# Root mean square of the output heads in a hybrid layer: column sums by matmul with tokens on partitions, instead of sums spread over channels

## The reference

```
y = jnp.concatenate([y_a, y_b, y_c, y_d.astype(x.dtype)], axis=-1).reshape(b, L, N_OUT_HEADS, HEAD_DIM)
y = rms_norm(y, w['out_norm'].reshape(N_OUT_HEADS, HEAD_DIM)).reshape(b, L, D_MIX)
x = x + g2 * (y @ w['w_out'])
```

## Time and profile before

| | |
|---|---|
| median of 3 runs | 2008.23 us (2001.43 to 2008.45) |
| profiled execution, its own time | 2006.56 us |
| span of that execution | 2004.7 us, so 1.9 us lie around it |
| mean granted TensorE clock | 0.915 of full speed |
| the stage of the norm, first layer | about 700 to 764 us |
| the same, second layer | about 1649 to 1709 us |

### The profile page before, as it was taken

One profiled execution on the slowest core, in us unless ns is written; L12 is line 12 of the kernel. 1 busy time (PEld: TensorE's weight loads), 2 busy tenths in 40 slices (PEclk: granted clock), 3 DMA queues, 4 the chain that ended last, 5 costly groups with the idle time before them and its releaser, 6 DMA issues.

```text
span 2004.7 us, 27629 instructions
## 1 busy us (share of the span) xinstructions
PE 1791.1 (89%) x11432; PEld 1520.4 (76%) x11432; DVE 978.6 (49%) x1755; ACT 585.5 (29%) x778; POOL 206.3 (10%) x373
## 2 busy tenths in 40 slices
PE   4888899999886899899997999989988688899998
PEld 2788888666664656799997999956766365589998
DVE  2443342356666673444435544235765756344443
ACT  2432331114221232433324433111423122244331
POOL 3000001520012400000000000062002140000000
PEclk8899999999866899899998999999986778989999
DMA  8545444867101156345442454484410115225442
GB/s 269 170 162 188 167 168 147 265 211 252 46 14 38 39 187 212 105 127 168 149 146 92 142 164 142 140 233 150 133 42 17 34 40 168 84 85 168 129 160 74
DMA packets 206089, 271.99 MB, mean 136 GB/s; under 512 B 11527, under 2 KB 182072, under 8 KB 205964
## 3 DMA queue, kind: packets, MB, share of 16 engines
q1 hardware_dynamic: 191760, 249.48, 37.7%
q0 software_dynamic: 13328, 20.65, 4.1%
q10 hardware_dynamic: 876, 0.09, 0.0%
HBM read 264.68 MB, written 5.50 MB: 135 GB/s over the span
## 4 chain that ended last, share of the span: by engine, by line
PE 77%; DVE 12%; DMA 6%; ACT 2%; issue 1%; ACTq 1%; SPq 1%; DVEq 0%
PE bank L764 14%; PE bank L766 14%; PE bank L765 14%; PE bank L873 10%; DMA sqk<-in_w_ada_dram 5%; PE bank L1262 4%; PE bank L1004 3%; PE bank L698 2%; PE bank L1159 2%; PE bank L997 1%; PE bank L1023 1%; PE bank L1171 1%; DVE big L2140 1%; PE bank L688 1%; DVE sq L2197 1%
## 5 line engine op out<-in xcount | busy, mean ns | idle before, releaser
L766 PE MATMUL bank<-hT_r,ring_r 128*128 128x320 f32 x1408 | 443.1, 315 | 0.0
L766 PEld LDWEIGHTS bank<-hT_r,ring_r 128*128 128x128 f32 x1408 | 269.8, 192 | 0.0
L764 PE MATMUL bank<-hT_r,lat_pages_r 128*128 128x320 f32 x704 | 220.9, 314 | 13.8 <-DVE gates_r L1592 13.6
L1575 DVE TENSOR_TENSOR ring_r<-ring,lat_pages_r 128x2048 fp32r<-128x2048 f32 (+1 forms) x68 | 151.5, 2230 | 149.5 <-ACT lat_pages_r L1288 149.5
L873 PE MATMUL bank<-hT,ring 128*128 128x320 f32 x736 | 214.4, 448 | 10.2 <-DVE hT L1588 10.2
L765 PE MATMUL bank<-gates_r,lat_pages_r 128*128 128x320 f32 x704 | 221.1, 314 | 0.0
L766 PE MATMUL bank<-big_r,ring_r 128*128 128x320 f32 x704 | 218.0, 310 | 0.0
L873 PEld LDWEIGHTS bank<-hT,ring 128*128 128x128 f32 x736 | 142.0, 196 | 73.4 <-issue 21.4
L1288 ACT ACTIVATE lat_pages_r<-ring 128x2048 fp32r<-128x2048 f32 (+1 forms) x68 | 126.5, 1862 | 128.0 <-PE bank L766 64.6
L764 PEld LDWEIGHTS bank<-hT_r,lat_pages_r 128*128 128x128 f32 x704 | 135.3, 192 | 19.6 <-issue 16.7
L765 PEld LDWEIGHTS bank<-gates_r,lat_pages_r 128*128 128x128 f32 x704 | 135.5, 192 | 0.0
(11 more groups left out here) (522 smaller groups left out, 3228.9 us busy)
## 6 DMA issues: line engine op xcount, KB each, us to landing
ring<-in_w_ffn_in_dram SPq DMA_DIRECT2D x88, 1024.0 KB, 5.4
ring<-in_w_ada_dram SPq DMA_DIRECT2D x56, 1024.0 KB, 5.4
ring<-in_w_ffn_out_dram SPq DMA_DIRECT2D x32, 1024.0 KB, 5.2
ring<-in_w_in_dram SPq DMA_DIRECT2D x22, 1024.0 KB, 7.3
sqk<-in_w_ada_dram SPq DMA_DIRECT2D x32, 512.0 KB, 8.5
ring<-in_w_ffn_out_dram SPq DMA_DIRECT2D x16, 768.0 KB, 4.7
lat_pages<-in_cache_mla_latent_dram POOLq DMA_DIRECT2D x128, 64.0 KB, 2.2
ring<-in_w_out_dram SPq DMA_DIRECT2D x8, 1024.0 KB, 8.1
```

The source lines that it names most:

```text
L764: mm(out, w_h, x_h, start=start, stop=False)
L766: return mm(out, w_l, x_h, start=False, stop=stop)
L1575: go(v.tensor_tensor(slot_r(n, nk, 256), slot(n, nk, 256), w_hi_r[g % HI][:, 0:nk].bitcast(F32), ALU.subtract), w_low)
```

## The change

The sums of a head are formed with tokens on partitions, for all chunks at once. `head_sums` makes the squares the stationary operand (128 channels x up to 128 tokens) and the two indicator columns `rows64` (128x2) the moving one, so that one small matmul gives two sums for every token: 22 such matmuls in part 0 and 2 in part 1 (the sample tokens of the last two chunks). The 48 columns of results lie in one bank. ACT takes the root with scale and eps in the same instruction (`head_root`), DVE takes the reciprocal of at most 128x32 values (`head_invert`), and `head_spread` brings the factors back to channels: the stationary operand is one factor column broadcast to 64 columns, the moving one the identity, six matmuls to a chunk. `scale` then reads the factor out of PSUM, chunk by chunk, in the ten parts of `SPREAD`. `BATCH` stays for the squares. The places of the steps in the streams of PE, ACT and DVE move as shown.

```diff
--- before.py
+++ after.py
@@ -94,14 +94,16 @@
 
 BATCH = [(0, 0, T), (2, 0, T), (4, 0, T), (6, 0, TP), (6, TP, T)]
 
+SPREAD = [(k, 0, T) for k in range(6)] + [(6, 0, TP), (7, 0, TP), (6, TP, T), (7, TP, T)]
+
 
 PER = {"states_loaded": 16 * 11, "pages_loaded0": 1024, "pages_loaded1": 1024, "proj_loaded": 16 * 7, "stored": 16 * 16,
        "stored_rows": 16 * 4, "turned": 2, "turned_used": 2, "out_ready": 5, "win_done": 25, "win_act": 10, "win_dve": 15,
        "conv_done": 1, "silu_conv": 1, "ssd_act_in": 3, "ssd_act": 6, "ssd_pe": 7, "ssd_dve": 8, "lru_pe": 2, "lru_act": 3,
        "lru_dve": 2, "hg_e": 8, "hg_bc": 8, "hg_pe": 9, "hg_dve": 7, "mla_pe": 12, "mla_act": 2, "mla_dve": 10,
        "cq_copied": 1, "att_t": 8, "att_tc": 8, "att_k": 32, "att_sq": 32, "att_in": 8, "att_rk": 8, "att_mix": 8,
-       "soft_pe": 12, "soft_dve": 20, "soft_act": 4, "group_used": 4, "on_pe": 5, "on_sq": 5, "on_inv": 5, "on_root": 5,
-       "on_scaled": 5, "wo_done": 8, "wo_used": 8, "mla_act_in": 2, "mla_root": 2, "prob_act": 8, "wkr_ready": 1,
+       "soft_pe": 12, "soft_dve": 20, "soft_act": 4, "group_used": 4, "on_pe": 2, "on_sq": 5, "on_inv": 2, "on_root": 2, "on_spread": 10,
+       "on_scaled": 10, "wo_done": 8, "wo_used": 8, "mla_act_in": 2, "mla_root": 2, "prob_act": 8, "wkr_ready": 1,
        "acol_taken": 1, "mixed": 5}
 
 
@@ -266,6 +268,8 @@
         pend = carve(ext, 1920, 2, NBLK + NB)
         kv_tok = carve(conv, 0, 3, 512)
         hg_s0 = carve(conv, 1536, 2, NB, 64)
+
+        head_inv = carve(ext, 0, KD, 3, 2)
 
         cq = carve(cqkr, 0, 2, T)
         ckv = carve(cqkr, 640, T)
@@ -422,6 +426,7 @@
         on_sq = sem("on_sq")
         on_inv = sem("on_inv")
         on_root = sem("on_root")
+        on_spread = sem("on_spread")
         on_scaled = sem("on_scaled")
         wo_done = sem("wo_done")
         wo_used = sem("wo_used")
@@ -1193,15 +1198,30 @@
                     from_states(1, 0).then_inc(hg_pe, 1)
                     from_states(2, 1).then_inc(hg_pe, 1)
 
-                    def out_norm(n):
-
-                        pe.wait_ge(on_sq, at(on_sq, n + 1))
-                        if n:
-                            pe.wait_ge(on_inv, at(on_inv, n))
-                        k0, c0, c1 = BATCH[n]
-                        for k in range(k0, k0 + 2):
-                            ins = mm(bank[2 + k % 2][:, c0:c1], c("ones64"), sqx[:, k, c0:c1], start=True, stop=True)
+                    def head_sums(part):
+
+                        pe.wait_ge(on_sq, at(on_sq, (4, 5)[part]))
+                        for k in range(0, KD) if part == 0 else (6, 7):
+                            for cc, (t0, L) in enumerate(TC):
+                                if part == (k > 5 and cc == 2):
+                                    ins = mm(bank[2][0:L, 6 * k + 2 * cc:6 * k + 2 * cc + 2], sqx[:, k, t0:t0 + L], c("rows64"),
+                                             start=True, stop=True)
                         ins.then_inc(on_pe, 1)
+
+                    def head_spread(*parts):
+
+                        for i in parts:
+                            k, c0, c1 = SPREAD[i]
+                            pe.wait_ge(on_inv, at(on_inv, 1 + i // 8))
+                            if i >= 2:
+                                pe.wait_ge(on_scaled, at(on_scaled, i - 1))
+                            for cc, (t0, L) in enumerate(TC):
+                                if c0 <= t0 < c1:
+                                    for h in range(2):
+                                        ins = mm(bank[2 + k % 2][64 * h:64 * h + 64, t0:t0 + L],
+                                                 head_inv[0:L, k, cc, h:h + 1].to_broadcast([L, 64]), c("ident", L)[:, 0:L],
+                                                 start=True, stop=True)
+                            ins.then_inc(on_spread, 1)
 
 
                     tail_tiles, tail_steps = iter(TAIL[l]), sorted({step for step, _ in TAIL[l]})
@@ -1216,21 +1236,21 @@
 
                     soft_turn(2)
                     soft_spread(2)
-                    out_norm(0)
+                    head_sums(0)
                     tail(1)
                     value(2)
                     value_taken(2)
                     turn(6)
-                    out_norm(1)
+                    head_spread(0, 1)
                     tail(1)
                     score(6)
                     tail(2)
-                    out_norm(2)
+                    head_spread(2, 3)
                     turn(7)
                     tail_turn(0)
                     tail(1)
                     score(7)
-                    out_norm(3)
+                    head_spread(4, 5)
                     tail(4)
                     soft_turn(3)
                     tail_turn(1)
@@ -1239,18 +1259,19 @@
                     tail(1)
                     value(3)
                     value_taken(3)
+                    head_spread(6, 7)
                     for h in range(4):
                         r = slice(64 * (h % 2), 64 * (h % 2) + 64)
                         ins = mm(bank[7][r, (h // 2) * 64:(h // 2) * 64 + 64], wukv[:, 1, h * 64:(h + 1) * 64],
                                  pn.rearrange("p b (h t) -> p b h t", h=4)[:, :, h], start=True, stop=True)
                     ins.then_inc(mla_pe, 1)
                     tail(3)
-                    out_norm(4)
+                    head_sums(1)
                     tail(2)
                     tail_turn(2)
-
-
-                    pe.wait_ge(on_scaled, at(on_scaled, 5))
+                    head_spread(8, 9)
+
+                    pe.wait_ge(on_scaled, at(on_scaled, 10))
                     for m in range(KD):
                         tile_ready(pe, pos["wout", l, m // 2])
                         w = slot(pos["wout", l, m // 2], 8, 256)
@@ -1517,29 +1538,31 @@
                         ac.wait_ge(mixed, at(mixed, n + 1))
                         o.go(f(batch(sqx, n), batch(hT, n), ACT.Square), on_sq)
 
-                    def on_sqrt(n):
-                        ac.wait_ge(on_inv, at(on_inv, n + 1))
-                        o.go(f(batch(sqx, n), batch(sqx, n), ACT.Sqrt), on_root)
+                    def head_root(part):
+                        ac.wait_ge(on_pe, at(on_pe, part + 1))
+                        sums = bank[2][:, 0:48].rearrange("p (k c h) -> p k c h", k=KD, c=3)
+                        if part == 0:
+                            o.go(f(head_inv[:, :, 0:2], sums[:, :, 0:2], ACT.Sqrt, bias=eps, scale=1.0 / 64))
+                            o.go(f(head_inv[0:64, 0:6, 2], sums[0:64, 0:6, 2], ACT.Sqrt, bias=eps[0:64], scale=1.0 / 64), on_root)
+                        else:
+                            o.go(f(head_inv[0:64, 6:8, 2], sums[0:64, 6:8, 2], ACT.Sqrt, bias=eps[0:64], scale=1.0 / 64), on_root)
 
                     for n in range(4):
                         on_square(n)
                     soft_exp(2)
-                    on_sqrt(0)
+                    head_root(0)
                     att_copy(6)
-                    on_sqrt(1)
                     att_squares(6)
                     att_root(6)
                     tail_copy(0)
                     att_copy(7)
-                    on_sqrt(2)
                     att_squares(7)
                     att_root(7)
                     tail_copy(1)
                     soft_exp(3)
-                    on_sqrt(3)
                     on_square(4)
                     tail_copy(2)
-                    on_sqrt(4)
+                    head_root(1)
                     tail_copy(3)
                     for k in range(KD):
                         square(3 * l + 2, k)
@@ -2188,47 +2211,43 @@
                         o.tell(mixed)
 
 
-                    def invert(n):
-                        k0, c0, c1 = BATCH[n]
-                        ve.wait_ge(on_pe, at(on_pe, n + 1))
-                        for k in range(k0, k0 + 2):
-                            go(v.tensor_scalar(sqx[:, k, c0:c1], bank[2 + k % 2][:, c0:c1], 1.0 / 64, EPS, MUL, ADD))
-                        o.settle()
-                        go(v.reciprocal(sqx[:, k0:k0 + 2, c0:c1], sqx[:, k0:k0 + 2, c0:c1]), on_inv)
-
-                    def scale(n):
-                        k0, c0, c1 = BATCH[n]
-                        ve.wait_ge(on_root, at(on_root, n + 1))
-                        for k in range(k0, k0 + 2):
+                    def head_invert(part):
+                        ve.wait_ge(on_root, at(on_root, part + 1))
+                        if part == 0:
+                            go(v.reciprocal(head_inv[:, :, 0:2], head_inv[:, :, 0:2]))
+                            go(v.reciprocal(head_inv[0:64, 0:6, 2], head_inv[0:64, 0:6, 2]), on_inv)
+                        else:
+                            go(v.reciprocal(head_inv[0:64, 6:8, 2], head_inv[0:64, 6:8, 2]), on_inv)
+
+                    def scale(*parts):
+                        for i in parts:
+                            k, c0, c1 = SPREAD[i]
```

(21 more changed lines are left out.)

## The result

The changed kernel takes 2025.91 us (median of five runs, 2021.08 to 2026.94), the kernel before 2008.23 us beside it (2001.43 to 2009.84). The ratio is 1.009, 95% interval 1.0076 to 1.0104: slower by 17.7 us, against a forecast of +14 on the median and +15.5 on the profiled execution. The profiled execution took 2026.78 us, its span 2025.1 us.

What follows compares the result with a forecast made beforehand. PE's own stream was taken as the bound, DVE's reciprocals mostly lying beside it. The terms gave +7.8 us in the first layer and +7.75 in the second, together +15.5 on 2006.56: 2022 us, range 2009 to 2029.

Steps and rivals of the forecast that it cites:

- Start of the sums: Sums on PE begin later because they wait for four squares instead of one: +0.9 us in both layers.
- Price of the sums: 22 two-column sum matmuls at half clock take 8.2 us where the old pair took 2.43: +5.8 us per layer.
- Clock behind the sums: From `tail` to the end of `value`, PE's clock rises 4.5 us after the sums end: +0.85 and +0.6 us.
- `turn(6)` and first spread, +0.4, and the score's wait, -1.3: Clock falls before `turn(6)`, two spreads cost more than the old pair; `score(6)` loses its 1.26 us wait for ACT's root.
- `score(6)` to `turn(7)`: PE's spread of chunk 2 newly waits for DVE's first `scale`; the stretch grows from 3.1 to 4.1 us: +0.95.
- `score(7)`: In the product of `score(7)`, a 0.3 us wait on ACT goes: -0.3 us.
- Before L1016 (the old L1011): Ahead of this line, waits mostly cover two spreads and `tail(4)`, or in layer two DVE's scales: -0.1 and +0.15 us.
- The last batch and its spreads: Up to `w_out`: spreads of chunks 6, 7 +1.2 and +0.9 us; shorter DMA backlog -0.6, shorter norm chain -0.35.
- A: Rival: the clock rises during the sums, as before at 706.5; total +7.4 us, 2014 us; chance 0.17.
- B: Rival: two columns nearly free, weights loading in other matmuls' shadow, sums 2.5 us; total +2.6 us, 2009 us; chance 0.10.
- C: Rival: DVE's reciprocals were the bound, about -10 to -15 us with cheap sums; 1994 us; chance 0.03.
- D: Rival: PE stays at half clock through `turn(6)`, spreads and `score(6)`, about 5 us more per layer; 2032 us; chance 0.10.

Runs made afterwards that it cites:

- one-sum kernel: Changed kernel with one broadcast matmul in place of part 0's 22 sum matmuls, output not the program's; 2006.5 us, ratio 1.0017 to the kernel before.
- two `scale(0, 1)` executions: Changed kernel with `scale(0, 1)` ahead of `att_inv(6)` on DVE, in a single run and then six; 2014.84 us, then 2020.26 us (ratio 1.0055 to the kernel before).
- 64 and 128 columns: Changed kernel with each sum matmul moving 64 or 128 columns instead of 2; 2032.46 and 2031.77 us, ratios 1.0125 and 1.0134 to the kernel before.
- late: Changed kernel with part 0's sums moved behind `value(2)` and `head_invert(0)` behind `soft_values(2)`; 2036.56 us, ratio 1.0159 to the kernel before.
- woven: Changed kernel with part 0's 22 sum matmuls issued one by one between wide matmuls of `tail(1)` and `value(2)`; 2053.83 us, ratio 1.0233 to the kernel before.

## Why the prediction was right, and where its sizes were off

The mechanism was the one forecast: PE's stream was the bound, the sums came out of it at the price of their weight loads at half clock, and DVE's reciprocals were cover. The total was 4 us low on the median and, by the spans, 4.9 us low on the profiled execution (+20.4 against +15.5). Of these 4.9 us the stages make 1.2; the other 3.7 lie outside them, where the forecast put nothing ("the shift stays"), and are within the scatter said above. The terms, measured from the last square's end in both traces:

- **Start of the sums:** forecast +0.9, measured +0.93. The wait is for ACT's squares, 0.87 us in the bracket.
- **Price of the sums:** forecast 8.2 us, measured 9.28; +6.85 instead of +5.8. The step that failed is "6 x 0.24 for the six with half as many weight columns". By the starts of its records a chunk of two 128-token pieces takes 0.86 us, so 0.43 a matmul as forecast, and a chunk of three 1.24, so the third piece adds 0.38 us where half the weight columns had been taken for 0.24. 16 x 0.43 + 6 x 0.38 = 9.2. Set alone between wide matmuls the short piece took 0.30 us and the full one 0.52. The bound of 8.4, L862 doubled, fell as well: it makes 0.38 us of a full piece that took 0.43.
- **Clock behind the sums:** forecast a rise 4.5 us after they end, within 3.3 to 5.4, and +0.85 and +0.6. Measured 5.4 us, and +1.5 and +1.2: the far end, which the kernel before had shown at this very place. Averaging it with the 3.3 of 426.7 was the error of size. That the rise is to be counted from the end of the sums at all is not borne out: with more moving columns it came 3.6 and 1.5 us after their end in the first layer, and always 14.2 or 14.7 us after their start.
- **`turn(6)` and first spread, +0.4, and the score's wait, -1.3:** together -0.9 forecast, -2.4 measured in both layers. The clock did not fall before `turn(6)` in this execution, which made 1.5 us. The wait itself is gone as forecast. In the one-sum kernel and in one stage each of the two `scale(0, 1)` executions it did fall, so this term is a matter of the execution, and that it went the right way here is luck.
- **`score(6)` to `turn(7)`:** forecast +0.95, measured +0.97 and +0.98. The wait of 0.60 us on the bank that `scale(0)` reads stands where it was put, and goes when `scale(0)` goes first.
- **`score(7)`:** forecast -0.3, measured -0.32 and -0.34.
- **Before L1016 (the old L1011):** forecast -0.1 and +0.15, measured -0.07 and -0.48. In the second layer the wait shrank from 1.60 to 0.37 us, more than PE's extra work.
- **The last batch and its spreads:** forecast +0.6 and +0.55, measured +1.2 and +1.35. In the first layer nothing was saved on the tile of `w_out`: the wait is 2.59 us where 2.48 was, so the allowance of -0.6 for a shorter DMA backlog had no basis. In the second the clock was at half, which the forecast had not allowed for, and the chain behind the last square took 1730.28 - 1727.31 = 2.97 us instead of 2.65. ACT's timeline shows the table load in it, as forecast:

```profile
1727.00 0.31 ACT L1539 ACTIVATE sq<-hT 128x128 f32<-128x128 f32 x1 [11.65 <-DVE hT L2248]
1727.32 1.28 ACT L1548 ACT_TABLE_LOAD   x1
1728.62 0.26 ACT L1548 ACTIVATE ext<-bank,small 64x4 f32<-64x4 f32 x1
```

The sum of the misses is small because they have both signs: -1.5 at `turn(6)` (and -0.6 before L1016 in the second layer) against +1.05 on the sums, +0.65 on the clock and +0.6 to +0.8 at the end, per layer. With the clock's fall at `turn(6)` that the forecast had assumed, the stages would have come out some 4 us above it and not 1; that they came so close is in part luck.

Of the signs given, DVE at 940 us came (939.4), `value(2)` ended 9.3 and 9.0 us later after the last square where 7 were forecast, and PE gained 28.3 us of busy time, not 15: 19.2 in the stages, since waits went as well as work came, and 9.1 outside. Two figures of the prediction are wrong in themselves: by the earlier trace rows the clock fell at 423.3 and not at 423.4, which changes nothing, and with 1.1 us of sums in place of 2.5 in both layers the estimate beside rival B comes to 2006.4 us and not to 2008.

Of the rivals, A (the clock rises during the sums) fell in every kernel that has them: with 2, 64 and 128 columns in this place all 44 records ran at half, and in the late place a clock that was full fell. B (the columns are nearly free) fell with the first row: 0.211 us a record. The Trainium skill's 25 ns for few columns ("TensorE: Matmul & The Clock Gate", section "Back-to-back issue gap") is a floor, and the estimate beside B took it for a price; where each matmul brings new 128x128 fp32 weights this trace has more than eight times that, at half clock. C (the reciprocals were the bound) is excluded by the one-sum kernel, which has no wide reciprocals and gained nothing. D did not come in the changed kernel, but in five of the variants: late and woven in both layers, one sum, 64 columns and the six runs of `scale(0, 1)` in the second (13.7, 13.7 and 10.2 us at half from `turn(6)` on). In the one-sum kernel, which had nothing else to lose, that stage was 4.8 us longer than before, the 5 us forecast for it.

## What to carry to other kernels

A matmul with data as the stationary operand and a handful of moving columns is paid by its weight load, here 0.43 us at half clock, whatever the few columns promise; put the constant block into the array and let the data move, which did the same sums in a fifth of the time. Before work is taken from a loaded engine, look in the bound engine's timeline for the gaps that this work causes: here 1.3 us per layer, which an exchange of two instructions removed without any new matmuls. The clock behind an insertion can change with it, so cost that stretch as well as the insertion. And where runs of one kernel lie 6 to 15 us apart, compare stages, and look whether the clock took the same course in them, before a difference of a few us is given a cause.

## What the runs showed of the hardware that was not expected

- Gapless fp32 matmuls that are bound by weight loads did not raise TensorE's clock here: PEclk stayed 0.50 through 9.3, 10.6 and 12.7 us of them, and fell from 1.00 inside them, 0.8 us after they began, when it had been high. In the first layer the rise came 5.4, 3.6 and 1.5 us after their end with 2, 64 and 128 columns, 14.7, 14.2 and 14.2 us after their start.
- At 1.2 GHz fp32 records with full 128x128 weights start 0.21 us apart with 2 and with 128 moving columns alike. Only where pieces with 64 weight columns stand between them do the columns add time: 0.21, 0.24 and 0.29 us a record on average for 2, 64 and 128 columns.
- A full-width sum set between matmuls of 32 weight columns cost 0.52 us, and made each of those cost 1.0 us instead of 0.23 in a row.
- The same gaps of 1.0 and 0.3 us around `turn(6)` come with a fall of the clock in one execution and without it in another. In the three executions with the changed kernel's stream on PE (its own and the two with `scale(0, 1)` first) it fell in two of six stages. Two of these second-layer stages, with and without the fall, are 70.3 and 64.2 us long. Such falls may be part of the 6 to 15 us by which runs of one kernel differ.
